# Sums of squares over the heads of the first mixer: two passes of the rounded format instead of a plain fp32 product

## The reference

```python
def _rms(x, g):
    xf = x.astype(jnp.float32)
    y = xf * lax.rsqrt(jnp.mean(xf * xf, axis=-1, keepdims=True) + EPS)
    return (y * g.astype(jnp.float32)).astype(x.dtype)

qa = _rms(_heads(a_q, A_HEADS), a_q_g)      # 8 heads of 64
ka = _rms(_heads(a_k, A_HEADS), a_k_g)
...
yc = jax.nn.silu(c_g.astype(f32)) * _rms(_merge(oc), g_c.reshape(C_HEADS, HEAD_DIM)).reshape(bsz, t, C_DIM)
```

## Time and profile before

| | before |
|---|---|
| runs, us | 1093.53, 1093.35, 1092.87 |
| median, us | 1093.35 |
| span of the profiled execution, us | 1091.2 |
| TensorE matmul busy, of the span | 99% |
| VectorE busy | 65% |
| ScalarE busy | 39% |

### The profile page before, as it was taken

The page is one execution under the profiler, slowest core; times in us unless marked ns, Lnnn a source line. Parts: engine busy times, 40 slices in busy tenths (PEclk is TensorE's granted clock), DMA queues, the critical chain, the costliest instruction groups (busy, mean ns, idle before and its releaser), DMA issues.

```text
span 1091.2 us, 13622 instructions
## 1 busy us (share of the span) xinstructions
PE 1078.4 (99%) x5409; PEld 868.7 (80%) x5411; DVE 713.4 (65%) x1142; ACT 421.6 (39%) x663; POOL 0.2 (0%) x4
## 2 busy tenths in 40 slices
PE   9999999999999999999999999999999999999997
PEld 6877877877878888888888888887776777888886
DVE  6897877868768887754488745654568446364431
ACT  6612555334352323222222234744357443323232
POOL 0000000000000000000000000000000000000000
PEclk9999999999999999999999999999999999999999
DMA  8432121131213223233422134333121222033302
GB/s 256 121 116 78 39 77 41 57 136 39 78 39 126 97 97 106 58 87 101 151 78 87 49 97 154 92 102 116 44 78 39 78 77 78 1 117 115 111 25 77
DMA packets 100240, 95.94 MB, mean 88 GB/s; under 512 B 5953, under 2 KB 91089, under 8 KB 100177
## 3 DMA queue, kind: packets, MB, share of 16 engines
q1 hardware_dynamic: 100000, 95.05, 27.2%
q10 hardware_dynamic: 176, 0.02, 0.0%
HBM read 92.95 MB, written 2.10 MB: 87 GB/s over the span
## 4 chain that ended last, share of the span: by engine, by line
PE 94%; DVE 3%; ACT 1%; issue 1%; DVEq 0%; ACTq 0%
PE ring L1031 23%; PE ring L1033 22%; PE ring L1032 22%; PE bank L1031 3%; PE bank L1033 3%; PE bank L1032 3%; PE bank L1486 1%; PE bank L1281 1%; PE bank L1253 1%; PE bank L1186 1%; PE bank L1266 1%; PE bank L1118 1%; PE bank L1510 1%; PE bank L1459 1%; PE ring L1349 1%
## 5 line engine op out<-in xcount | busy, mean ns | idle before, releaser
L1031 PE MATMUL ring<-act_hi,w_hi 128*128 128x512 f32 (+1 forms) x816 | 323.5, 396 | 0.9 <-DVE xT L2302 0.5
L1033 PE MATMUL ring<-act_hi,w_lo 128*128 128x512 f32 (+1 forms) x816 | 316.7, 388 | 0.0
L1032 PE MATMUL ring<-act_lo,w_hi 128*128 128x512 f32 (+1 forms) x816 | 316.4, 388 | 0.0
L1574 ACT ACTIVATE w_hi<-w_raw 128x2048 fp32r<-128x2048 f32 (+4 forms) x97 | 160.9, 1659 | 248.1 <-PE ring L1033 212.8
L1918 DVE TENSOR_TENSOR w_lo<-w_raw,w_hi 128x2048 fp32r<-128x2048 f32 (+5 forms) x102 | 191.4, 1879 | 4.0 <-ACT w_hi L1574 3.7
L1031 PEld LDWEIGHTS ring<-act_hi,w_hi 128*128 128x128 f32 x816 | 153.3, 188 | 37.4 <-issue 3.9
L1032 PEld LDWEIGHTS ring<-act_lo,w_hi 128*128 128x128 f32 x816 | 153.3, 188 | 31.8 <-issue 1.9
L1033 PEld LDWEIGHTS ring<-act_hi,w_lo 128*128 128x128 f32 x816 | 153.2, 188 | 31.7
L1033 PE MATMUL ring<-hidH,w_lo 128*128 128x512 f32 x176 | 68.5, 389 | 0.0
L1031 PE MATMUL ring<-hidH,w_hi 128*128 128x512 f32 x176 | 68.5, 389 | 0.0
L1032 PE MATMUL ring<-hidL,w_hi 128*128 128x512 f32 x176 | 68.5, 389 | 0.0
(11 more groups left out here) (360 smaller groups left out, 1624.4 us busy)
## 6 DMA issues: line engine op xcount, KB each, us to landing
w_raw<-in_w_in SPq DMA_DIRECT2D x30, 1024.0 KB, 5.1
w_raw<-in_w_up SPq DMA_DIRECT2D x22, 1024.0 KB, 5.0
w_raw<-in_w_out SPq DMA_DIRECT2D x8, 1024.0 KB, 5.0
w_raw<-in_w_down SPq DMA_DIRECT2D x8, 768.0 KB, 4.6
w_raw<-in_w_down SPq DMA_DIRECT2D x8, 640.0 KB, 4.3
w_raw<-in_w_in SPq DMA_DIRECT2D x7, 512.0 KB, 5.8
xin<-in_xt SPq DMA_DIRECT2D x8, 256.0 KB, 4.2
xT<-in_xt SPq DMA_DIRECT2D x2, 1024.0 KB, 6.6
```

What stands on the lines that cost most here:

```text
L1031: pe.matmul(out, ah, bh, start=(first and n == 0), stop=False)
L1032: pe.matmul(out, ah, bl, start=False, stop=False)
L1033: mm = pe.matmul(out, al, bh, start=False, stop=(last and n == len(pairs) - 1))
L1574: return act.activation(out, src, func, **more)
```

## The change

The ten products become two passes each. ScalarE writes the square twice, once rounded (sqH, fp32r) and once in fp32 (scr). VectorE, which had nothing to do in hg_sq and qk_sq, subtracts the one from the other into sqL (fp32r). TensorE multiplies blkR, a rounded copy of blk, by sqH and then by sqL into the same bank, with a wait for VectorE's subtraction (nrm_lo) between the two. ScalarE makes blkR once, in hg_sq 0, behind its wait for hg_o. The lists of stages are unchanged. Two semaphores (lb_d and nbcf_ready) become one, lb_nbcf.

```diff
+        sqH = [sb(f"sqH{i}", [P, T], F32R, M + 22 + 2 * i) for i in range(2)]
+        sqL = [sb(f"sqL{i}", [P, T], F32R, M + (20, 26)[i]) for i in range(2)]
+        blkR = sb("blkR", [P, P], F32R, M + 10)
...
-                    pe.matmul(nrm_bank(n)[:], cc("blk"), scr[n % 2][:], start=True, stop=True).then_inc(nrm_mm, 1)
+                    pe.matmul(nrm_bank(n)[:], blkR[:], sqH[n % 2][:], start=True, stop=False)
+                    pe.wait_ge(nrm_lo, n + 1)
+                    pe.matmul(nrm_bank(n)[:], blkR[:], sqL[n % 2][:], start=False, stop=True).then_inc(nrm_mm, 1)
...
-                    act.wait_ge(lb_d, 1)
+                    act.wait_ge(lb_nbcf, 1)
...
-                    act.wait_ge(nbcf_ready, 1)
+                    act.wait_ge(lb_nbcf, 2)
...
                     if kind == "hg_sq":
                         act.wait_ge(hg_o_mm, i + 1)
-                        for hh in range(2):
-                            r = slice(64 * hh, 64 * hh + 64)
-                            ins = A(scr[n % 2][r, :], bank[2 * i + hh][r, :], ACT.Square)
+                        if i == 0:
+                            A(blkR[:], cc("blk"), ACT.Identity)
+                        for to in (sqH[n % 2], scr[n % 2]):
+                            for hh in range(2):
+                                r = slice(64 * hh, 64 * hh + 64)
+                                ins = A(to[r, :], bank[2 * i + hh][r, :], ACT.Square)
                         ins.then_inc(nrm_sq, 1)
                     else:
...
                         act.wait_ge(z_in, z_at[of])
+                        A(sqH[n % 2][:], src, ACT.Square)
                         A(scr[n % 2][:], src, ACT.Square).then_inc(nrm_sq, 1)
...
-                    TT(lbd, pc("lb", 0, 2), pc("lb", 0, 2), ALU.subtract).then_inc(lb_d, 1)
-                    TS(nbcf, pc("b_cf", 0, 2), -1.0, None, ALU.mult).then_inc(nbcf_ready, 1)
+                    TT(lbd, pc("lb", 0, 2), pc("lb", 0, 2), ALU.subtract).then_inc(lb_nbcf, 1)
+                    TS(nbcf, pc("b_cf", 0, 2), -1.0, None, ALU.mult).then_inc(lb_nbcf, 1)
...
+                elif kind in ("hg_sq", "qk_sq"):
+                    n = s[1] + (2 if kind == "qk_sq" else 0)
+                    dve.wait_ge(nrm_sq, n + 1)
+                    if n >= 2:
+                        dve.wait_ge(nrm_mm, n - 1)
+                    TT(sqL[n % 2][:], scr[n % 2][:], sqH[n % 2][:], ALU.subtract).then_inc(nrm_lo, 1)
                 elif kind == "hg_y":
```

More of the change, by code:

```diff
@@ L128, in two_blocks @@
             sem(n) for n in ("x_sq", "x_sum", "x_ss", "x_rs", "x_hi", "x_lo", "x_col", "z_in"))
-        lb_d, lb_e, nbcf_ready, mask_ready = (sem(n) for n in ("lb_d", "lb_e", "nbcf_ready", "mask_ready"))
+        lb_nbcf, lb_e, mask_ready = (sem(n) for n in ("lb_nbcf", "lb_e", "mask_ready"))
         gate_ln, gate_m, gate_rows, gate_cols, negC_ready, negB_in = (
@@ L139, in two_blocks @@
             sem(n) for n in ("hg_kd", "hg_cross_mm", "hg_sc", "hg_u_mm", "hg_u_s", "hg_scan", "hg_rep_mm", "hg_dm", "hg_in_mm", "hg_o_mm", "hg_n", "hg_done"))
-        nrm_sq, nrm_mm, nrm_rs, nrm_done, qk_done = (sem(n) for n in ("nrm_sq", "nrm_mm", "nrm_rs", "nrm_done", "qk_done"))
+        nrm_sq, nrm_lo, nrm_mm, nrm_rs, nrm_done, qk_done = (sem(n) for n in ("nrm_sq", "nrm_lo", "nrm_mm", "nrm_rs", "nrm_done", "qk_done"))
         conv_b, qkB_ready, ml_m_mm, ml_w, ml_e, ml_s_mm, ml_p, ml_o_mm, ml_o_s = (
```

## The result

| | before | after |
|---|---|---|
| median of the runs, us | 1093.11 | 1104.12 (1103.18 to 1105.19) |
| span of the profiled execution, us | 1091.2 | 1101.7 |
| TensorE, VectorE, ScalarE busy, us | 1078.4, 713.4, 421.6 | 1081.6, 719.7, 428.3 |

The ratio is 1.0100, with a 95% interval of 1.0087 to 1.0113: the change costs 11 us. The work added is about what was forecast: 6.3 us on VectorE for 6.9 (ten subtractions, part of each overlapping its neighbour) and 6.7 us on ScalarE, for which the prediction writes 6.3 while its own terms add up to 6.9. The kernel of each experiment has numbers of its own.

A forecast was written before the change was run, and what follows sets the result against it. TensorE, busy 99% of the span, was taken as the bound. Waits of 2.7 + 1.4 + 1.1 + 1.5 + 1.75 + 3.7 = 12.2 us, less 4.2 saved, gave +8.0: 1093.35 becomes 1101.3 us, range 1096.0 to 1105.0.

The forecast's parts named there:

- lag of gate_math: VectorE, stopped at hg_sq for ScalarE's second squares and its own subtractions, starts gate_math 7.4 us later than before.
- wait 1: At hg_sq VectorE's stop delays the drain of b_o 1, so TensorE waits 2.7 us to open a_q 1.
- wait 2: The first product with the norm slips on VectorE, so TensorE waits 1.4 us for the drain of a_q 0.
- product 2: One of the ten products of heads' sums: TensorE waits 1.1 us for ScalarE's second square and VectorE's subtraction.
- ml_s 0: Its last score waits for VectorE's first PM product, costing TensorE 1.5 us.
- product 6: One of the ten products: a late second square and subtraction make TensorE wait 1.75 us.
- product 9: VectorE must first make the norm queued ahead of the last subtraction, so TensorE waits 3.7 us.
- attention: Stage behind the ten products: its first scores start near 209 instead of 201.03, +8.0 us.
- The saving: Two rounded passes replace each fp32 product on TensorE: 0.415 us saved each, 4.2 us for ten.
- the clock rival: TensorE's waits of 2.7 or 3.7 us drop its clock to 1.2 GHz, +2 to +4 on top: 1104.3, chance 0.13.
- rival "faster": Saving stands and waits are covered if VectorE's lag at gate_math stays under 4.7 us: 1089.2, chance 0.06.
- Nothing gives it back: From attention's start, TensorE, VectorE and ScalarE carry about the same lag, so the +8.0 us stays to the end.

The follow-up runs named there:

- e7: The change with each qk square one product earlier on ScalarE and the ten subtractions on GpSimd instead of VectorE: 1090.15 us, ratio 0.9970.
- e5: The change with the rounded high half alone: one square and one pass per sum, no VectorE part, low half left out: 1088.99 us, ratio 0.9962.
- e4: The change with 12 unused passes on TensorE filling the wait ahead of the second pass of product 9: 1100.99 us, ratio 1.0069.
- e2: The change with only the eight qk products in two rounded passes, the two hg products plain with single squares: 1100.00 us, ratio 1.0060.
- e11: The change in its own order, with the ten subtractions made by GpSimd instead of VectorE: 1096.07 us, ratio 1.0026.
- e8: The change with unused passes on TensorE in both long waits, 11 ahead of a_q 1 and 12 in product 9: 1100.45 us, ratio 1.0064.
- e9: The kernel before, with only a VectorE wait in hg_sq for ScalarE's single square added: 1093.46 us, ratio 1.0002.
- e10: The kernel before with VectorE's wait in hg_sq and ScalarE's hg squares made twice, no subtraction, plain products: 1095.72 us, ratio 1.0022.
- e1: The change with only the two hg products in two rounded passes, the eight of a_q and a_k plain: 1096.26 us, ratio 1.0027.
- e3: The change with VectorE's two hg subtractions moved behind the drain of b_o 1 instead of ahead of gate_math: 1099.46 us, ratio 1.0056.

## Why the prediction was right, and where it wasn't

The direction, the mechanism and the places held. The waits one by one, the measured ones by the distance from start to start less what it was before, with the saving of the product in between added:

| | forecast | measured |
|---|---|---|
| lag of gate_math, from the drain of b_o 0 | 7.4 | 7.4 |
| wait 1, drain of b_o 1 | 2.7 | 2.8 |
| wait 2, drain of a_q 0 | 1.4 | 1.6, as slower passes |
| product 2 | 1.1 | 0.9 |
| ml_s 0 | 1.5 | 1.5 |
| product 6 | 1.75 | 1.7 |
| product 9 | 3.7 | 3.7 |
| attention | +8.0 | +8.1 |

The measured waits add up to 12.2 us, less 4.2 saved, as the forecast ones do. The single terms are off by up to 0.2 either way and cancel, which is partly luck.

**The saving.** 0.415 us a product was the right size: where nothing waits (e7), ten of them bring attention forward by 4.1 us. That all of it reaches the end was not: 3.3 us do in e7. The prediction's sentence that each microsecond taken from TensorE is worth one holds for the stretch and not for the start of attention behind it; there TensorE begins to wait for VectorE (e7, e5). Of the 1.0 us lost there, 0.7 are the two waits named at e7; the rest wasn't followed up.

**The sum was short by 3 us,** and the step that failed is the weighing of the clock rival. It had a chance of 0.13 and the time 1104.3; the measured time is 1104.12, and e4 shows that it is this mechanism: with the last wait filled, 1100.99, next to the forecast of 1101.3. I had argued from the end of the trace, where the clock stayed up for over 3 us behind the last matmul (4.0 by the trace: the last matmul ended at 1085.1), that waits of 2.7 and 3.7 us are probably short enough. In the change it fell at the end of the first long wait and 1.1 us behind the end of the second, in e2 inside that wait, and in e11 behind waits of 1.3 and 0.85 us close to each other. One fall at one place says little on when it comes; a mostly idle stretch of this length should have been given even odds or more. What the rule cited from the Trainium skill (TensorE: Matmul & The Clock Gate, Why this matters for your kernels) said, that gaps bring the half rate back, is what happened, and by it the time would have been met to 0.2 us. The gaps that the row there speaks of are longer, though, than the 2.6 us of idle time measured here; the measurement decides.

**The price of a fall depends on what stands behind it.** The first one costs nothing (e8 against e4): TensorE, at half rate for some 3.4 us, only uses up wait 2. The second costs 3.0 us at yt, since attention starts at full load. My "+2 to +4, of which VectorE's lag hides a part" was right for the sum of both.

**The deciding point of the rival "faster"** was put at the wrong drain. I said that VectorE's lag at gate_math has to stay under 4.7 us. e9 has 4.7 without any saving, for which the drain of b_o 1 would allow 5.1, and TensorE waits 1.0 us, at the drain of a_q 0. The point is there: before, that drain ended at 135.67 and TensorE wanted the bank at 137.94, 2.3 us of room; with the 1.3 us that VectorE gives back at hg_y 0, a lag of 3.6 at gate_math is the most that costs nothing, and 0.4 less where product 0 is shortened. e9, at 4.7, exceeds it by 1.1, and waits 1.0 us. The rival's condition was thus too lenient by 1.5 us; with a lag of 7.4 that changed nothing. The same slip returned in the expectation of e10.

**"Nothing gives it back"** was nearly right: in the runs that are late at yt, 0.5 to 0.8 us less are left at the end of the span, except for e11, where it is 0.3 more. That part stays open.

## What to carry to other kernels

A helper instruction in an in-order queue costs what stands behind it, not its own time: the same ten subtractions stand in a kernel 11 us slower than before as the change places them, 1.7 us faster where VectorE has idle time and the producer is a product ahead, and 3.3 us faster with those early squares and the subtractions on an idle engine. Before adding a wait to an engine with much idle time, list what is queued behind it up to the next thing that the bounding engine needs (here two drains), and compare the stop with the least room among them, not with the first. And count waits of TensorE twice when several fall together or one is long: once for themselves, and once for the lower clock behind them, if full work stands there.

## What the runs showed of the hardware that was not expected

The granted clock falls for shorter idle times of TensorE in mid kernel than at the end of it, where it fell 4.0 us behind the last matmul. It was at 2.4 GHz in e9 (one wait of 1.0 us) and e10 (waits of 1.4 and 1.2 us, one tile apart) throughout; it fell to 1.2 GHz at or behind each single wait of 2.6 us (the change, e1, e2, e3, e4) and in e11 behind 1.3 and 0.85 us that follow each other. Once down it stayed there for 3.4 to 10 us, with TensorE at full work most of that time, and for unlike lengths behind the same wait: some 7 us in the change and in e3, some 10 in e2. Where waits are near the point, executions of one program differ: e11 ran from 1094.4 to 1100.3 us, e9, with no fall in its profile, from 1093.3 to 1093.7.

GpSimd's fp32 subtraction of 128x512 took 1.3 us in the median of e7, not quite twice VectorE's 0.69, and 1.6 in that of e11, with single ones up to 2.15. Drains from the ring (128x512, one operand in PSUM) kept their 0.69 us beside it; some instructions on SBUF alone didn't: a copy of 4x512 took 1.34 us for 0.42, a TENSOR_SCALAR of 4x512 1.40 for 0.42, a subtraction of 8x512 1.73 for 0.68, and in e11 one of 128x512 (yL) 1.78 for 0.68. An idle engine's help isn't free for the engine beside it, even where, as in e7, the time gains.
